# Attention by pairs of heads in both halves of the rows, with normed probabilities and values summed in PSUM

## The chip, the cores and the metric

The kernel runs on one core of a Trainium2 chip. The metric is device time in microseconds (us) of one execution; every program is executed several times and the median counts. TensorE (PE) multiplies matrices from SBUF into PSUM, VectorE (DVE) and ScalarE (ACT) work element by element, GpSimd (POOL) here issues gathers by index, SyncE (SP) issues the loads of the weights. Each engine works through its own queue in program order, and the queues meet at semaphores.

## The reference, cut to what matters

Two transformer blocks follow each other on 512 tokens of width 1024, in float32.

- The first block has MLA attention (8 heads, 96 wide keys, 16 meta tokens ahead of the sequence), a retention branch, a merge by sigmoid gates, and then PEER: each token picks 128 rows of a table `peer_u` of 16384 rows, takes the dot product of each with its activations, and adds 128 rows of a table `peer_v`, weighted, to the residual.
- The second block has a pooling branch, an attention of three branches (NSA), gates, and an MLP of width 4096.

The NSA part is the larger share of what is changed:

```
s = jnp.where(mask, (q @ k.T) * scale, -1e30); p = where(mask, softmax(s), 0)
o_c = p_c @ v_cmp          # compressed keys: at most 31, one softmax
o_s = p_s @ v_sel          # with 512 tokens every block is selected: causal attention
o_w = p_w @ v_win          # the window holds all 512 tokens: causal attention
o = g[0] * o_c + g[1] * o_s + g[2] * o_w    # 16 heads, 2 groups of keys, head width 64
```

The MLA part is `o = softmax(mask(q @ k.T * scale)) @ v` for 8 heads of value width 64.

## The kernel before

The 512 tokens are four tiles of 128. `first_wave` (L1766) runs the first block on tiles 0 and 1 (run 0) and on tiles 2 and 3 (run 1). `second_wave` (L1925) runs the second block on tiles 0 and 1 (run 0), tile 2 (run 1) and tile 3 (run 2). Within a wave the stages follow one another (norm, products, rope, turning, attention, merge, MLP). A stage begins on an engine once the last work of the stage before has ended on all engines (`open`, `begin`). Weights stream through a ring of three slabs of 2 MB, loaded by SP.

The PEER picks of the first block are spread over later stages. There are 1024 steps of VectorE (4 tiles, 128 rows of `peer_u` and 128 of `peer_v` each). Each step needs one gather of 128 rows of 4 KB, issued by POOL (L306) into one of 8 buffers. `SHARES` says how many steps each stage takes, and `g.picks.use(dve)` puts a stage's steps evenly between its own instructions on VectorE. Tiles 0 and 1 must be complete (512 steps) before run 0 of the second wave, tile 2 (892 steps) before run 1 and tile 3 (1024) before run 2. Run 2 of the second wave has no picks. `on_pe` is False for all, so that VectorE does each of them: L363 for `peer_u`, L369 for `peer_v`.

`attention_stage` (L784 to L953) takes a list of items. An item is one head, one query tile and one branch. Its steps are:

- TensorE: scores (L835, queries stationary), one more product that adds the mask (L836, identity times a causal bias), for MLA also 16 meta columns (L840).
- VectorE: the maximum of the scores (L931). ScalarE: exponential with the sum of the row (L890). VectorE: for the compressed branch a product with `seen` (L936).
- TensorE: transposes of the unnormed probabilities, 128 keys each (L875). ScalarE: copies them to SBUF (L899, L902).
- TensorE: values, the turned probabilities stationary (128 columns), the values moving (64 columns) (L865). Each item has its own sum in PSUM.
- VectorE: reciprocal of the sums (L911), gate (L913), and then factor times values, added to the head's output (L918, L920).

The output has tokens in the rows, so that one more `turn_stage` ("to") turns it for the merge. Item i's scores lie in one of three banks (in one of two places where there are more than 512 keys, which is called wide, tile 3 of MLA). For NSA a head's items are compressed, selected, window. There are 48 items for a tile of the second wave and 8 for one of the first. The keys of a tile t are 128 (t + 1) in number.

## Time and profile before

| | us |
|---|---|
| time, median of 3 runs | 3436.53 (3432.90 to 3439.03) |
| profiled execution, own time | 3432.37 |
| its span | 3431.0 |
| PE busy | 2454.4 (72%) |
| DVE busy | 1890.6 (55%) |
| ACT busy | 456.1 (13%) |
| POOL busy | 1311.4 (38%) |
| gathers (queue q0) | 148416 packets, 539.79 MB for 1024 gathers |
| weight loads (queue q1) | 283.19 MB |

The span is from the first to the last instruction of the program. Busy shares are averages over stages with different limits, so that they say little by themselves. The mean granted TensorE clock over the span is 0.734 of full speed. Full speed is 2.4 GHz and the lower level is 1.2 GHz.

### The profile page before, as it was taken

The page shows a single profiled execution, that of the slowest core. Times are in us where ns is not written, and L with a number is a line of the kernel's source. Part 1 is how long each engine was busy: PE and PEld are TensorE (multiplying, and loading weights), DVE is VectorE, ACT ScalarE, POOL GpSimd, SP SyncE. Part 2 cuts the span into 40 slices and gives each one's busy share as a digit, 9 for nine tenths or more (in the row PEclk, how much of TensorE's full clock was granted, in tenths as well). Part 3 has the DMA queues.
Part 4 walks back from the last instruction along what each step waited for, and adds up shares of the span by engine and source line. Part 5 has one row for each costly group of instructions (what it writes and reads, how often), then busy time and mean ns, then how long its engine had stood idle before and what let it go on. Part 6 is the DMA issues. An engine that isn't in the chain of part 4 may idle for free. (4 is left out here: it accounts for less than half of the span.)

```text
span 3431.0 us, 24950 instructions
## 1 busy us (share of the span) xinstructions
PE 2454.4 (72%) x8300; PEld 1594.3 (46%) x8300; DVE 1890.6 (55%) x3669; ACT 456.1 (13%) x1214; POOL 1311.4 (38%) x1041
## 2 busy tenths in 40 slices
PE   6998930365847543003959998897679979799989
PEld 3547630234526522002647686763356534466544
DVE  1511169887676778997777656666554442212100
ACT  1201000012101000000023210110122100122110
POOL 0000004767466877347664345885431241000000
PEclk9998965685767866555855579999755789855699
DMA  4221406898688999669897569999863699510176
GB/s 138 92 85 65 162 21 196 308 384 294 225 338 285 402 331 363 194 209 335 327 352 226 174 234 400 371 401 401 308 228 90 212 398 336 189 37 0 63 268 226
DMA packets 291711, 829.17 MB, mean 242 GB/s; under 512 B 23568, under 2 KB 30144, under 8 KB 290816
## 3 DMA queue, kind: packets, MB, share of 16 engines
q0 software_dynamic: 148416, 539.79, 43.8%
q1 hardware_dynamic: 139872, 283.19, 22.7%
q10 hardware_dynamic: 3296, 4.60, 0.4%
q8 instruction: 67, 1.10, 0.1%
q14 instruction: 60, 0.49, 0.0%
HBM read 825.40 MB, written 2.10 MB: 241 GB/s over the span
## 5 line engine op out<-in xcount | busy, mean ns | idle before, releaser
L306 POOL DMA_INDIRECT picks_rows<-peer_u_dram,expert x512 | 698.2, 1364 | 821.0 <-DVE expert L1441 506.1
L306 POOL DMA_INDIRECT picks_rows<-peer_v_dram,expert x512 | 605.7, 1183 | 770.1 <-DVE h L369 655.6
L363 DVE CUSTOM_DVE_ANT_0 picks_rows<-picks_rows,xn 128x1024 f32<-128x1024 f32 x512 | 616.7, 1223 | 178.8 <-DMA picks_rows<-peer_u_dram,expert 173.7
L369 DVE SCALAR_TENSOR_TENSOR h<-picks_rows,picks_weight,h 128x1024 f32<-128x1024 f32 x512 | 655.0, 1279 | 101.5 <-ACT aT L2031 47.7
L637 PE MATMUL psum<-identity_sb,n_scaled 128*128 128x128 f32 (+1 forms) x104 | 23.6, 405 | 327.0 <-DVE n_scaled L622 327.0
L447 PE MATMUL psum<-weight_ring,hnT 128*128 128x512 f32 (+4 forms) x576 | 238.6, 576 | 23.5 <-DMA weight_ring<-w_in_dram 11.9
L1727 PE MATMUL psum<-weight_ring,aT 128*128 128x512 f32 x512 | 224.4, 600 | 8.6 <-DMA weight_ring<-w_ff_dram 6.4
L931 DVE TENSOR_REDUCE na_negmax<-psum 128x1 f32<-128x15 f32 (+6 forms) x192 | 74.3, 387 | 254.6 <-PE psum L836 254.4
L835 PE MATMUL psum<-nsa_kT_sb,qT 64*128 64x128 f32 (+3 forms) x256 | 181.2, 809 | 0.0
L447 PEld LDWEIGHTS psum<-weight_ring,hnT 128*128 128x128 f32 (+1 forms) x576 | 106.9, 188 | 153.8 <-issue 140.4
L637 PEld LDWEIGHTS psum<-identity_sb,n_scaled 128*128 128x128 f32 (+1 forms) x104 | 19.4, 218 | 332.7 <-issue 293.0
L1727 PEld LDWEIGHTS psum<-weight_ring,aT 128*128 128x128 f32 x512 | 97.8, 192 | 133.6 <-issue 121.0
L865 PE MATMUL psum<-nsa_kv_sb,na_probsT 128*128 128x64 f32 x640 | 157.3, 413 | 0.0
L865 PEld LDWEIGHTS psum<-nsa_kv_sb,na_probsT 128*128 128x128 f32 x640 | 151.5, 333 | 0.0
L447 PE MATMUL psum<-weight_ring,mergedT 128*128 128x512 f32 x256 | 115.6, 613 | 36.0 <-DVE mergedT L1192 34.6
L836 PEld LDWEIGHTS psum<-causal_sb,identity_sb 128*128 128x128 f32 x320 | 78.9, 296 | 121.7 <-issue 120.3
L1387 PE MATMUL psum<-keysT_sb,pqT 64*128 64x128 f32 x128 | 11.7, 352 | 172.4 <-DVE gates_sb L1447 171.5
L1309 PE MATMUL psum<-weight_ring,xn 128*128 128x512 f32 x256 | 120.3, 627 | 14.7 <-DMA weight_ring<-w_ff_dram 9.7
L890 ACT ACTIVATE na_probs<-psum,na_negmax 128x15 f32<-128x15 f32 (+6 forms) x192 | 85.2, 444 | 328.2 <-DVE na_negmax L931 327.9
L875 PE MATMUL psum<-identity_sb,na_probs 128*128 128x128 f32 (+2 forms) x384 | 125.3, 430 | 0.8 <-ACT na_probs L890 0.8
L447 PE MATMUL psum<-xn,weight_ring 128*128 128x256 f32 x512 | 113.0, 384 | 7.2 <-DVE xn L603 7.2
L1157 PE MATMUL psum<-hnT,weight_ring 128*128 128x256 f32 x512 | 115.6, 388 | 1.6 <-DVE oT L693 0.9
(357 smaller groups left out, 3422.4 us busy)
## 6 DMA issues: line engine op xcount, KB each, us to landing
weight_ring<-w_ff_dram SPq DMA_DIRECT2D x48, 2048.0 KB, 16.0
weight_ring<-w_in_dram SPq DMA_DIRECT2D x44, 2048.0 KB, 13.2
weight_ring<-w_proj_nsa_dram SPq DMA_DIRECT2D x6, 2048.0 KB, 7.9
weight_ring<-w_out_dram SPq DMA_DIRECT2D x6, 2048.0 KB, 18.7
weight_ring<-w_ret_out_dram SPq DMA_DIRECT2D x4, 2048.0 KB, 7.9
weight_ring<-w_mix_out_dram SPq DMA_DIRECT2D x4, 2048.0 KB, 18.2
weight_ring<-w_peer_q_dram SPq DMA_DIRECT2D x4, 2048.0 KB, 13.2
picks_rows<-peer_u_dram,expert POOLq DMA_INDIRECT x512, 9.3
```

The source lines that it names most:

```text
L306: pool.indirect_dma_start(out=self.rows[:, n % GATHERS, :], out_offset=None, in_=table, in_offset=bass.IndirectOffsetOnAxis(ap=self.expert ...
L363: ins = nc.vector.tensor_tensor_reduce(out=row, in0=row, in1=self.x[t], scale=1.0, scalar=0.0, op0=ALU.mult, op1=ALU.add, accum_out=self.d ...
L369: ins = nc.vector.scalar_tensor_tensor(out=h, in0=row, scalar=self.weight[:, t % 2, k:k + 1], in1=h, op0=ALU.mult, op1=ALU.add)
L447: mm = g.nc.tensor.matmul(g.psum[0:rows, n % BANKS, 0:cols], lhsT, rhs, start=(k == 0), stop=(k == len(pairs) - 1))
L835: nc.tensor.matmul(scores(i)[:, at:end], it.q, it.kT, start=True, stop=False)
L836: return nc.tensor.matmul(scores(i)[:, end - it.bias.shape[1]:end], g.identity[:], it.bias, start=False, stop=True)
L865: mm = nc.tensor.matmul(values(j), probsT[0:keys, j % 2, P * m:P * m + P], v, start=(m == 0), stop=(m == last))
L875: mm = nc.tensor.transpose(turned(j, m, keys), probs[:, j % depth, col:col + keys], g.identity[:])
L890: nc.scalar.activation(probs[:, i % depth, 0:items[i].keys], scores(i), ACT.Exp, bias=negmax[:, i % 4:i % 4 + 1], accum_out=rowsum[:, i % ...
L1157: mm = nc.tensor.matmul(g.psum[0:rows, n % BANKS, 0:cols], lhsT, rhs, start=(k == 0), stop=(k == len(pairs) - 1))
L1309: mm = nc.tensor.matmul(g.psum[:, n % 3, :], lhsT, rhs, start=(k == 0), stop=(k == len(pairs) - 1))
L1727: mm = nc.tensor.matmul(g.psum[:, n_tiles * b + t, :], aT[:, KT * k + i, P * t:P * t + P], w[:, i, :], start=(k == 0 and i == 0), stop=(k ...
```

## The change

- Items come in pairs: heads h and h + 1 of the same branch. For NSA the even head's queries and keys lie in SBUF rows 0 to 63, the odd head's in rows 64 to 127 (queries are turned two heads at a time, keys are turned twice).
- Queries are scaled by a negative number. One VectorE instruction (`tensor_tensor_reduce`) adds the mask to the scores in PSUM, in place, and takes their minimum. The product with the bias on TensorE is gone. ScalarE takes exp(-s + minimum).
- VectorE norms the probabilities in SBUF (reciprocal, then times factor and gate) ahead of the transposes.
- In the value products the values are stationary (64 columns) and the turned probabilities move (128 columns). The output comes out turned, head h in half h % 2 of the rows, and the three branches are summed in PSUM. A set of 8 heads (for MLA one tile's 8 heads) is evacuated by one ScalarE copy. The "to" stages are gone.
- Scores have four banks (two pairs) and probabilities four buffers. The wide case keeps two places.
- `SHARES` has new numbers: for run 1 of the first wave and `sel2`, `sel3` the sum stays 460, for run 0 and run 1 of the second wave 380 and 132. `compress_stage` and `mlp_down_stage` put picks at more places. `Picks.fold` and the extra `picks.add` calls do nothing here, since `on_pe` stays False.

```diff
 SHARES = {
-    "sel1": 24, "n1_1": 14, "lat_1": 19, "nq_1": 9, "nkv_1": 10, "up_1": 19, "qk_1": 19, "tq_1": 5, "tk_1": 6, "ma2_1": 28,
-    "ma3_1": 28, "rp_1": 43, "tr_1": 7, "re_1": 19, "rn_1": 8, "to_1": 4, "m1_1": 71, "mix_1": 24, "np_1": 14, "pq_1": 28,
-    "sel2": 43, "sel3": 42, "drain_0": 28, "n22_0": 8, "u2_0": 9, "pool2_0": 6, "q2_0": 17, "kc2_0": 8, "kv2_0": 11,
-    "cmp2_0": 31, "tq2_0": 4, "tk2_0": 2, "na2_0": 89, "to2_0": 3, "m2_0": 42, "out2_0": 13, "n32_0": 9, "ff12_0": 61,
-    "ff22_0": 60, "nf2_0": 7, "n22_1": 2, "u2_1": 4, "pool2_1": 2, "q2_1": 6, "kc2_1": 3, "kv2_1": 3, "cmp2_1": 17,
-    "tq2_1": 2, "tk2_1": 1, "na2_1": 29, "to2_1": 1, "m2_1": 16, "out2_1": 4, "n32_1": 3, "ff12_1": 18, "ff22_1": 19,
-    "nf2_1": 2}
+    "sel1": 24, "n1_1": 13, "lat_1": 13, "nq_1": 9, "nkv_1": 9, "up_1": 12, "qk_1": 16, "tq_1": 6, "tk_1": 5, "ma2_1": 26,
+    "ma3_1": 27, "rp_1": 35, "tr_1": 7, "re_1": 58, "rn_1": 9, "m1_1": 55, "mix_1": 18, "np_1": 22, "pq_1": 18, "sel2": 51,
+    "sel3": 51, "drain_0": 28, "n22_0": 11, "u2_0": 7, "pool2_0": 11, "q2_0": 14, "kc2_0": 9, "kv2_0": 15, "cmp2_0": 41,
+    "tq2_0": 7, "tk2_0": 3, "na2_0": 81, "m2_0": 46, "out2_0": 14, "n32_0": 11, "ff12_0": 50, "ff22_0": 49, "nf2_0": 11,
+    "n22_1": 4, "u2_1": 3, "pool2_1": 5, "q2_1": 5, "kc2_1": 3, "kv2_1": 4, "cmp2_1": 24, "tq2_1": 3, "tk2_1": 1,
+    "na2_1": 35, "m2_1": 10, "out2_1": 3, "n32_1": 5, "ff12_1": 11, "ff22_1": 12, "nf2_1": 4}
...
+def turn_twice(g, bank, columns, src, rows):
+    for part in (0, HD):
+        mm = g.nc.tensor.matmul(g.psum[part:part + HD, bank, columns], src, g.identity[0:rows, 0:rows], start=True, stop=True)
+    return mm
...
-def attention_stage(g, tag, items, head_dim, group):
+def attention_stage(g, tag, items, outputs):
...
-    depth = 2 if wide else 3
+    depth = 2 if wide else 4
...
+        def score(pe, s):
+            for i in pair(s):
+                it = items[i]
+                if i >= depth:
+                    pe.wait_ge(*s_exp.after(i - depth + 1))
+                    if wide:
+                        pe.wait_ge(*s_copied.after(i - depth + 1))
+                mm = nc.tensor.matmul(scores(i)[:, 0:it.kT.shape[-1]], it.q, it.kT, start=True, stop=True)
+                if it.meta is not None:
+                    mm = nc.tensor.matmul(scores(i)[:, it.kT.shape[-1]:it.keys], it.q, it.meta[0], start=True, stop=True)
+                mm.then_inc(s_scores.sem, 1)
+        def turn(pe, s):
+            for j in pair(s):
+                pe.wait_ge(*s_normed.after(j + 1))
+                if j >= 2:
+                    pe.wait_ge(*s_copied.after(j - 1))
+                for m, (at, keys, _) in enumerate(items[j].blocks):
+                    mm = nc.tensor.transpose(turned(j, m, keys), probs[:, j % 4, at:at + keys], g.identity[:])
+                mm.then_inc(s_turned.sem, 1)
+        def value(pe, s):
+            for j in pair(s):
+                it = items[j]
+                pe.wait_ge(*s_copied.after(j + 1))
+                if it.set >= 2 and items[j - 1].set < it.set:
+                    pe.wait_ge(*s_out.after(it.set - 1))
+                for m, (_, keys, v) in enumerate(it.blocks):
+                    mm = nc.tensor.matmul(values(j), v, probsT[0:keys, j % 4, P * m:P * m + P], start=it.start and m == 0,
+                                          stop=it.stop and m == len(it.blocks) - 1)
+                mm.then_inc(s_values.sem, 1)
...
+            for s in range(steps + 2):
+                if wide:
+                    turn(pe, s - 1)
+                    score(pe, s)
+                else:
+                    score(pe, s)
+                    turn(pe, s - 1)
+                value(pe, s - 2)
...
+            for s in range(steps + 4):          # ScalarE
+                if wide:
+                    copies(act, s - 1)
+                    exponentials(act, s)
+                else:
+                    exponentials(act, s)
+                    copies(act, s - 1)
...
+            for s in range(steps):              # VectorE
+                for i in pair(s):
                     dve.wait_ge(*s_scores.after(i + 1))
+                    nc.vector.tensor_tensor_reduce(out=scores(i), in0=scores(i), in1=items[i].mask, scale=1.0, scalar=-LOWEST,
+                                                   op0=ALU.add, op1=ALU.min, accum_out=least[:, i % 8:i % 8 + 1]).then_inc(s_least.sem, 1)
+                g.picks.use(dve)
+                for i in pair(s):
+                    it, p = items[i], probs[:, i % 4, 0:items[i].keys]
+                    f = factor[:, i % 8:i % 8 + 1]
+                    dve.wait_ge(*s_exp.after(i + 1))
+                    if it.seen is not None:
+                        nc.vector.tensor_tensor(p, p, it.seen, ALU.mult)
+                    link(nc.vector.reciprocal(f, rowsum[:, i % 8:i % 8 + 1]))
+                    if it.gate is None:
+                        ins = nc.vector.tensor_scalar(p, p, f, None, ALU.mult)
+                    else:
+                        ins = nc.vector.tensor_scalar(p, p, f, it.gate, ALU.mult, ALU.mult)
+                    ins.then_inc(s_normed.sem, 1)
                 g.picks.use(dve)
...
-                turn_stage(g, tag("tq"), [([q[:, j, HD * h:HD * h + HD] for h in range(h0, h0 + 4)], P,
-                                           qT[:, h0:h0 + 4, P * j:P * j + P]) for j in range(n) for h0 in range(0, NH, 4)],
-                           HD, scale=HD ** -0.5)
+                turn_stage(g, tag("tq"), [([q[:, j, P * c:P * c + P] for c in range(c0, c0 + 4)], P,
+                                           qT[:, c0:c0 + 4, P * j:P * j + P]) for j in range(n) for c0 in (0, 4)],
+                           P, scale=-HD ** -0.5)
...
-        turn_stage(g, tag("to"), [([o[:, j, P * c:P * c + P] for c in range(c0, c0 + 4)], P, oT[:, c0:c0 + 4, P * j:P * j + P])
-                                  for j in range(n) for c0 in (0, 4)], P)
```

## Rows read from the trace of the kernel before

**Rows 1.** Page, second part: granted clock in tenths, 40 slices of 85.8 us.

```profile
PEclk9998965685767866555855579999755789855699
```

**Rows 2.** Windows: us; PE, PEld, DVE, ACT, POOL busy (count); clock, DMA share, GB/s.

```profile
122.80:153.90 31.10, 29.65 (x217) 26.61 (x217) 11.10 (x40) 16.51 (x65) 0.00 (x0) 1.00 0.01 5
768.50:836.70 68.20, 40.03 (x147) 31.36 (x148) 51.05 (x68) 13.93 (x36) 52.42 (x40) 0.55 0.90 313
836.70:902.90 66.20, 47.91 (x167) 37.26 (x165) 43.03 (x48) 11.36 (x32) 35.51 (x28) 0.50 0.67 223
1765.70:1999.00 233.30, 232.16 (x768) 165.20 (x768) 166.30 (x412) 73.80 (x292) 90.72 (x92) 0.51 0.68 211
2527.20:2695.40 168.20, 167.04 (x528) 111.92 (x529) 73.97 (x175) 48.51 (x146) 28.09 (x30) 0.51 0.34 102
3025.50:3228.00 202.50, 201.33 (x625) 132.65 (x626) 44.31 (x144) 55.40 (x146) 0.00 (x0) 0.51 0.00 1
```

**Rows 3.** Timeline, last attention stage: start, us, engine, instruction, idle before.

```profile
3105.06 0.69 ACT L890 ACTIVATE na_probs<-psum,na_negmax 128x512 f32<-128x512 f32 x1 [2.87 <-DVE na_negmax L931]
...
3106.04 0.63 PE L835 MATMUL psum<-k_cmpT_sb,qT 64*128 64x31 f32 x2
...
3107.05 1.95 PE L865 MATMUL psum<-nsa_kv_sb,na_probsT 128*128 128x64 f32 x8
3108.79 1.06 PE L875 MATMUL psum<-identity_sb,na_probs 128*128 128x128 f32 x4
3109.78 2.07 PE L835 MATMUL psum<-nsa_kT_sb,qT 64*128 64x512 f32 x2
3111.78 0.80 PE L836 MATMUL psum<-causal_sb,identity_sb 128*128 128x128 f32 x2
```

**Rows 4.** Timeline after the last attention: the merge's first product.

```profile
3230.83 2.04 PE L1238 MATMUL psum<-weight_ring,h2T 128*128 128x512 f32 x2 [0.93 <-DVE oT L693]
```

**Rows 5.** VectorE groups by form: count, busy us, mean ns, idle before.

```profile
L363 DVE DVE_READ_ACCUMULATOR2_ANT picks_dots<- 128x1 f32 x512 | 41.5, 81 | 0.0
L931 DVE TENSOR_REDUCE na_negmax<-psum 128x1 f32<-128x512 f32 x32 | 22.1, 690 | 98.1 <-PE psum L836 98.1
L911 DVE RECIPROCAL na_factor<-na_rowsum 128x3 f32<-128x3 f32 x64 | 10.8, 169 | 0.0
L622 DVE TENSOR_SCALAR n_scaled<-h,n_inverse 128x1024 f32<-128x1024 f32 x12 | 9.0, 751 | 0.2
L622 DVE TENSOR_SCALAR nkv_scaled<-ckv,nkv_inverse 128x256 f32<-128x256 f32 x4 | 1.4, 345 | 0.0
```

**Rows 6.** Page, fifth part: the two instructions of the picks.

```profile
L363 DVE CUSTOM_DVE_ANT_0 picks_rows<-picks_rows,xn 128x1024 f32<-128x1024 f32 x512 | 616.7, 1223 | 178.8 <-DMA picks_rows<-peer_u_dram,expert 173.7
L369 DVE SCALAR_TENSOR_TENSOR h<-picks_rows,picks_weight,h 128x1024 f32<-128x1024 f32 x512 | 655.0, 1279 | 101.5 <-ACT aT L2031 47.7
```

**Rows 7.** Timeline of TensorE: retention's products by halves of columns and rows.

```profile
1011.67 1.49 PE L1027 MATMUL psum<-rv,rk 128*64 128x128 f32 x12
1013.09 2.08 PE L1011 MATMUL psum<-xn 64*128 64x128 f32 x16
```

**Rows 8.** Windows with the clock: compression, turning of queries, the stretch after.

```profile
1703.70:1757.30 53.60, 19.40 (x100) 18.99 (x100) 39.44 (x72) 0.59 (x3) 43.45 (x33) 0.50 1.03 404
...
1757.40:1761.40 4.00, 4.00 (x20) 3.33 (x21) 3.93 (x7) 2.24 (x4) 3.39 (x3) 0.50 1.03 411
1761.50:1768.20 6.70, 4.92 (x34) 3.78 (x32) 3.57 (x8) 4.53 (x9) 5.17 (x6) 1.00 1.01 388
```

**Rows 9.** Windows: retention run 1, merge run 1, MLP run 1, selection of tiles 2, 3.

```profile
997.70:1050.00 52.30, 29.05 (x112) 20.90 (x112) 36.26 (x74) 7.50 (x19) 23.63 (x20) 0.50 0.57 196
1067.10:1208.60 141.50, 104.69 (x450) 87.64 (x450) 94.78 (x169) 7.42 (x17) 107.74 (x73) 0.87 0.99 376
2782.00:2909.70 127.70, 110.77 (x258) 49.60 (x259) 49.23 (x41) 8.79 (x16) 41.18 (x33) 0.92 0.96 358
...
1327.80:1523.10 195.30, 3.79 (x32) 3.52 (x32) 190.17 (x489) 1.59 (x2) 94.13 (x87) 0.50 0.74 243
```

313 lines of the change are left out of this document (135 added, 178 removed).

## The prediction

> **What bounds the kernel now.** I read the granted clock in slices first, then windows of each attention stage, then the order of instructions inside the longest one, then the stages that hold the picks. Counted from 1, slices 21 to 23, 30, 31, 36 and 37 have the clock at half, among others [rows 1], and these are the three NSA attentions. The windows say how they are bound [rows 2]. The three NSA stages take 233.3, 168.2 and 202.5 us, 604 us or 18% of the span, TensorE is busy in all but 1 us of each, and the clock is 0.51, which is the 1.2 GHz level. VectorE is busy 71%, 44% and 22% of them. The MLA stages take 31.1 us (clock 1.00) and 68.2 + 66.2 us, in which picks on VectorE and TensorE take turns.
>
> Inside the last NSA stage [rows 3] an item with 512 keys costs on TensorE 2.00 us of scores, 0.6 of mask, 1.0 of transposes and 1.74 to 1.95 of values, some 5.5; a compressed item costs about 1.6. A head is two of the first and one of the second, 12.7 us, and 16 heads are 203 us, as the window has it. The value products are short of work: 64 moving columns for 128 loaded ones, so that each key block costs 0.22 us per instruction, the time of its load; in this window the loads alone are busy 132.65 us [rows 2].
>
> Elsewhere there are two kinds of stage, which matter for the new shares [rows 9]. In the merge and the MLP of run 1 the DMA share is 0.99 and 0.96: a gather more is 0.527 MB (539.79 MB / 1024) at about 400 GB/s, 1.31 us. In the selection VectorE is busy 190 of 195 us: a step more is what it costs there, 1.22 + 0.08 us for peer_u [rows 5, 6] or 1.28 us for peer_v [rows 6], I take 1.34 with the few hundredths between two.
>
> **The change part by part, at the low clock first.** *Mask product.* It goes: 0.6 us per item of 512 keys.
>
> *Scores.* Two heads stand in different halves of the rows. Eight score products of 128 columns that alternate so in the retention take 2.08 us in 16 instructions [rows 7]; an instruction with 512 moving columns takes 0.87 at the low clock (2.00 us for two, less 0.25 of loading [rows 3]), one with 128 a quarter, so that the 16 would take 3.5 us one after the other. Neighbours in different halves overlap, those in the same half do not. A pair has only two products of two parts each: part two of the first runs beside part one of the second, so that three of four parts are paid. At 512 keys: 3 × 0.87 + 0.25 for the first load = 2.85 us, against 4.0 [rows 3]. Without overlap it is 3.7; with full overlap 2.0. I take 2.85. MLA has 96 rows and gets nothing.
>
> *Transposes.* As before, 4 in 1.06 us [rows 3], 2.2 us for the pair.
>
> *Values.* 128 columns now move past 64 loaded ones, the form of the retention's products into halves of columns, 12 instructions in 1.49 us where halves alternate [rows 7], which is 0.25 us per product. Here the blocks of one head follow each other in one half. Bounds per block are 0.25 and 0.44 us (today's two instructions); I take 0.44, since only one boundary in eight changes the half. 8 × 0.44 = 3.5 us for the pair, no gain at the low clock, but the engine now streams all the time instead of waiting for loads.
>
> So a pair at 512 keys costs 8.6 us against 11.1, a compressed pair about 2.6 against 3.2 (0.63 us for the score [rows 3], less its mask), two heads 19.8 against 25.3. At the low clock the last stage would be 8 × 19.8 + 3 = 161 us.
>
> *The clock.* Does it stay low? In today's attention and in the compression (30 to 62 moving columns behind loads of 128, clock 0.50 over 53.6 us [rows 8]) the engine mostly waits for loads. Just after the compression the queries are turned, transposes of 128 moving columns behind 64 loaded, PE busy 4.00 of 4.00 us, and the clock goes from 0.50 to 1.00 in the next stretch [rows 8]. The new value products have that same shape. MLA run 0 keeps clock 1.00 with 29.65 of 31.10 us busy [rows 2]. I take it that the last NSA stage and the one before it run at the high level. The Trainium skill says otherwise of part of this work (TensorE: Matmul & The Clock Gate, Part 4): transposes in PE mode do not count as activity that lifts the clock. This trace speaks against it by the 0.50 to 1.00 above; if the page were right, the low clock of the first rival would be likelier than I have it.
>
> *VectorE.* The pass with the mask is not in the trace in this form (PSUM in and out). From below it is the reduction of 512, 0.69 us, from above one picks step of 1024 elements, 1.30 us [rows 5, 6]; I take 0.69 + 0.08 for the accumulator, and 1.04 ns less per element below 512. Norming is a reciprocal, 0.17, and a product in SBUF: 0.345 us for 256 and 0.751 for 1024 elements [rows 5] give 0.21 + n/1.9 ns, 0.48 at 512. With `seen` on the compressed items, 0.17 more, two heads of own VectorE work come to 7.9, 7.1, 6.2 and 5.5 us for 4, 3, 2 and 1 key blocks. Output factors and additions go.
>
> **Stage by stage.** *NSA, run 2* (no picks): at the high clock TensorE needs 9.9 us per two heads. A step on VectorE is pass, exponential (0.69 us [rows 3] and 0.19 for its sum), norm: 3.3 us at 512 keys, 8.6 per two heads with the serial waits, and it runs beside the transposes and values of the pairs before. TensorE sets the pace: 8 × 9.9 + 6 of filling and draining = 85 us, −117.
>
> *NSA, run 1*: 35 picks × 1.34 = 47 and 8 × 7.1 = 57 on VectorE, 104 us; TensorE needs 63 at the high and 126 at the low clock. VectorE sets the pace: 112 us, −56.
>
> *NSA, run 0*: 81 × 1.34 = 109 and 8 × (6.2 + 5.5) = 94, 203 us, and 7 for waits; TensorE at the low clock needs 8 × (11.8 + 8.5) = 162, hidden. 210 us, −23.
>
> *MLA, run 1*: tile 2, own work and 26 picks, 4 periods of 11.3 plus filling, 50 us. Tile 3 is wide: no scores of the next pair before this pair's copies, 4 × 13 + 10 = 62. Together 112 against 134.4, −22. *MLA, run 0*: 4 × 2.1 (VectorE with its waits for the exponential) + 4 × 3.0 (TensorE) + 5 = 25.5, −5.6.
>
> *"to" stages.* The last one puts the merge 3 us after the window's end at 3228.0 [rows 4]. Five of them with their picks apart: −2.4 (run 0), −4.4, −2.6, −2.9, and one of 4 picks in run 1, below. Turning queries in pairs saves 1 us in the last run; keys turned twice cost 0.6 each, hidden but there.
>
> *New shares.* Until `sel3` 65 steps move: 58 go from stages bound by the DMA or by TensorE with it (1.3 us each, −75), 4 with "to" (−4.6), 3 from attention (counted); retention takes 39 (+40: today 52.3 us with VectorE busy 36.3 [rows 9], then 58 × 1.34 + 12.7 = 90), selection 17 (+23), norms 9 (+12). Net −5. Run 0: compression takes 10 at DMA share 1.03 (+13 [rows 8]), other small stages 28 (+23, many beside TensorE), while MLP and products give 27, of which only the second MLP half is held by the DMA (−20): +16. Run 1: +20 for compression and small stages, −22 for merge and MLP, whose 127.7 us are 37 gathers and 32 MB of weights at 400 GB/s [rows 9]; 14 fewer leave 113: −2.
>
> **Sum.** Start −8. First wave run 1 −22 − 5 = −27. Second wave run 0: −23 − 4.4 + 16 = −11. Run 1: −56 − 2.6 − 2 = −61. Run 2: −117 − 2.9 − 1 = −121. Together −228 us. The profiled execution had 3432.4 us with a span of 3431.0; it would have 3204. The median of before is 4 us above it, 3436.5, so I forecast 3208.
>
> **Rivals.**
> 1. *The clock stays low.* For it: all three NSA stages had it low with TensorE busy throughout [rows 2]. Against it: the rise on transposes. Run 2 161 instead of 85, run 1 128 instead of 112: 3208 + 92 = 3300.
> 2. *The shares give nothing back.* Stages that lose picks are held by their products, while those that get picks pay in full. For it: the merge has TensorE busy 104.7 of 141.5 us and the MLP 110.8 of 127.7 [rows 9]. Against it: their DMA shares. The give-backs are 75 + 20 + 20: up to 3323.
> 3. *The hand-over becomes serial (slower).* Each pair goes VectorE, ScalarE, VectorE, TensorE, ScalarE, TensorE, and picks stand in front of the norm. If TensorE waits for normed probabilities at every step, its time adds to VectorE's instead of lying beneath it: run 0 203 + 162 (+155 on my value), run 1 104 + 126 (+118), run 2 63 + 158 (+136), MLA +30: 3208 + 439 = 3647. It decides (3436) once half of TensorE's work is uncovered. Against it: four score banks hold two pairs, and between scores and transposes of a pair lie some 4 us of other TensorE work at the high clock, more than the 3.3 us that are waited for.
> 4. *More comes back than I count*, as whole stages have slack today (first wave run 1 above all): 60 us more, 3148.
>
> **Chances.** Forecast 0.60, rival 1 0.15, rival 2 0.11, rival 3 0.03, rival 4 0.11. The forecast's own range is 3160 to 3250; eight in ten needs both neighbours: 3130 to 3305. A difference of 0.2% (7 us) is about what a measurement of this kernel can tell from no change. Faster 0.95, same 0.01, slower 0.04.
>
> **What would show it.** The windows of the three NSA attentions near 210, 112 and 85 us; clock about 1.00 in the last; no line for the mask product; score pairs starting within one part of each other; the pass over 512 scores near 0.77 us; retention of run 1 near 90 us and merge of run 1 near 120. I am wrong if the last attention takes over 130 us, if TensorE there idles before the transposes, or if the time saved in attention reappears in stages that got picks.

## The result and the profile after

| | us | ratio to before, 95% interval |
|---|---|---|
| before, median | 3437.78 | |
| after, median of 4 runs (3161.86 to 3182.18) | 3173.71 | 0.9228 (0.9193 to 0.9262) |
| after, 6 more runs beside the experiments (3157.44 to 3183.50) | 3172.89 | 0.9217 (0.9177 to 0.9257) |

The change makes the kernel 7.7% faster, 264 us. The forecast was 3208, the range 3130 to 3305. The six further runs are called the control below. The profiled execution of after took 3182.18 us with a span of 3180.8, 250 less than the span of before. Its clock in slices, which stands against [rows 1], and its windows of the five attention stages, then of retention and merge in run 1 (columns as in [rows 2]):

```profile
PEclk9787995577585896655585557989987698986999
```

```profile
121.90:172.30 50.40, 48.58 (x184) 32.68 (x184) 13.50 (x64) 15.89 (x67) 0.00 (x0) 0.54 0.01 4
751.20:874.90 123.70, 76.08 (x280) 51.66 (x280) 93.03 (x155) 26.08 (x69) 88.85 (x64) 0.57 0.85 294
1774.10:1957.60 183.50, 118.35 (x576) 62.06 (x576) 170.69 (x520) 63.37 (x296) 120.83 (x92) 0.53 0.81 263
2481.70:2579.80 98.10, 73.04 (x432) 45.86 (x432) 86.73 (x244) 41.12 (x148) 41.08 (x37) 0.74 0.69 211
2891.50:2980.50 89.00, 79.06 (x528) 53.22 (x528) 54.01 (x208) 48.23 (x147) 0.00 (x0) 0.83 0.00 1
...
956.70:1047.90 91.20, 29.05 (x112) 20.91 (x112) 85.62 (x116) 7.50 (x19) 65.65 (x57) 0.50 0.92 334
1059.20:1172.80 113.60, 99.37 (x448) 86.89 (x449) 72.90 (x131) 7.41 (x17) 82.83 (x58) 0.94 0.99 375
```

Set against [rows 2], this is where the time went, in this profile and in the control's, which shows the same kernel in another execution:

| stage | before | forecast | after | control |
|---|---|---|---|---|
| MLA run 0 | 31.1 | 25.5 | 50.4 | 45.7 |
| MLA run 1 | 134.4 | 112 | 123.7 | 115.0 |
| NSA run 0 | 233.3 | 210 | 183.5 | 181.3 |
| NSA run 1 | 168.2 | 112 | 98.1 | 97.9 |
| NSA run 2 | 202.5 | 85 | 89.0 | 85.9 |
| the five together, difference | | -225 | -225 | -244 |
| all the rest, difference | | -3 | -25 | -16 |

That forecast and profile agree at -225 is chance: the five terms are off by +25, +12, -27, -14 and +4 us, which cancel, and the control's sum is another.

TensorE was the bound of all three NSA stages. Now VectorE is that of run 0 (busy 170.7 of 183.5) and run 1 (86.7 of 98.1), and in run 2 nobody is busy throughout: TensorE 79 of 89 us, VectorE 54.

The rest comes apart by the starts and ends of the windows. From MLA run 0 to MLA run 1 it is 614.6 us before and 578.9 after (fewer picks there), from MLA run 1 to NSA run 0 862.8 and 899.2 (more picks), from the end of NSA run 1 to the start of run 2 330.1 and 311.7. Retention in run 1 went from 52.3 to 91.2 us and the merge to 113.6, as the picks moved: near 90 and 120 were forecast.

### The profile page after: what moved, and what is told of

It is laid out like the page before. It is cut to its first block and busy times, and to the rows that moved or that the text cites. A ratio compares the mean times of both kernels' runs of the same rounds, so it can differ in the third digit from the quotient of the medians.

```text
span 3180.8 us, 23856 instructions
## 1 busy us (share of the span) xinstructions
PE 2103.0 (66%) x7838; PEld 1321.1 (42%) x7838; DVE 1912.1 (60%) x3970; ACT 425.6 (13%) x1209; POOL 1346.1 (42%) x1041
## 3 DMA queue, kind: packets, MB, share of 16 engines
q8 instruction: 63, 1.03, 0.1%
## 5 line engine op out<-in xcount | busy, mean ns | idle before, releaser
L315 POOL DMA_INDIRECT picks_rows<-peer_v_dram,expert x512 | 636.3, 1243 | 561.7 <-DVE h L380 451.4
L874 PE MATMUL psum<-identity_sb,na_probs 128*128 128x128 f32 (+2 forms) x384 | 93.7, 360 | 99.8 <-DVE na_probs L958 78.5
L1333 PE MATMUL psum<-weight_ring,xn 128*128 128x512 f32 x256 | 118.8, 621 | 11.6 <-DVE xn L621 7.4
L874 PEld LDWEIGHTS psum<-identity_sb,na_probs 128*128 128x128 f32 (+2 forms) x384 | 48.8, 160 | 161.2 <-DVE na_probs L958 148.6
L945 DVE CUSTOM_DVE_ANT_0 psum<-psum,mask_sb 128x128 f32<-128x128 f32 (+7 forms) x160 | 76.5, 514 | 57.2 <-PE psum L865 33.7
L907 ACT ACTIVATE na_probs<-psum,na_least 128x15 f32<-128x15 f32 (+6 forms) x192 | 83.5, 440 | 193.6 <-DVE na_least L945 193.5
L1181 PEld LDWEIGHTS psum<-hnT,weight_ring 128*128 128x128 f32 x512 | 100.2, 196 | 20.0 <-ACT xn L1140 5.8
L465 PEld LDWEIGHTS psum<-xn,weight_ring 128*128 128x128 f32 x512 | 98.5, 193 | 22.7 <-issue 9.3
```

What stands on the lines that cost most here:

```text
L315: pool.indirect_dma_start(out=self.rows[:, n % GATHERS, :], out_offset=None, in_=table, in_offset=bass.IndirectOffsetOnAxis(ap=self.expert ...
L465: mm = g.nc.tensor.matmul(g.psum[0:rows, n % BANKS, 0:cols], lhsT, rhs, start=(k == 0), stop=(k == len(pairs) - 1))
L874: mm = nc.tensor.transpose(turned(j, m, keys), probs[:, j % 4, at:at + keys], g.identity[:])
L907: nc.scalar.activation(probs[:, i % 4, 0:items[i].keys], scores(i), ACT.Exp, bias=least[:, i % 8:i % 8 + 1], scale=-1.0, accum_out=rowsum[ ...
L945: nc.vector.tensor_tensor_reduce(out=scores(i), in0=scores(i), in1=items[i].mask, scale=1.0, scalar=-LOWEST, op0=ALU.add, op1=ALU.min, acc ...
L1181: mm = nc.tensor.matmul(g.psum[0:rows, n % BANKS, 0:cols], lhsT, rhs, start=(k == 0), stop=(k == len(pairs) - 1))
```

## The experiments

All times are medians, and each ratio is to the kernel before on the same chip. Ratios from different chips are compared with their intervals. A window of a stage is cut as in [rows 2], from TensorE's first product of it to its end.

**New shares alone**, in the kernel before.

```diff
 SHARES = {
-    "sel1": 24, "n1_1": 14, "lat_1": 19, "nq_1": 9, "nkv_1": 10, "up_1": 19, "qk_1": 19, "tq_1": 5, "tk_1": 6, "ma2_1": 28,
+    "sel1": 24, "n1_1": 13, "lat_1": 13, "nq_1": 9, "nkv_1": 9, "up_1": 12, "qk_1": 16, "tq_1": 6, "tk_1": 5, "ma2_1": 26,
...
```

> The kernel before with nothing changed but SHARES, which take the changed kernel's numbers. Theory (as in the prediction): stages that lose picks and stages that get them nearly cancel, -5 and +16 and -2 us by the prediction's sum, and the picks that move in or out of the NSA attentions cost nothing there, as TensorE sets the pace of those stages in the kernel before. So 3437 + 9 = 3446 us, at most 20 either way. Rival 1: the new shares are a large part of the gain by themselves, 40 us or more faster than before. Rival 2: they only fit the new attention, and the old one with them is 40 us or more slower.

Measured: 3441.83 us, ratio 1.0001 (0.9972 to 1.0031). The theory holds; the new shares alone give nothing beyond 10 us. But the profile showed something else. Window of MLA run 0:

```profile
119.60:172.90 53.30, 52.23 (x216) 45.68 (x216) 10.83 (x39) 16.80 (x65) 0.00 (x0) 0.52 0.01 4
122.80:172.90 50.10, 50.08 (x198) 43.60 (x198) 9.90 (x36) 15.02 (x62) 0.00 (x0) 0.50 0.00 1
```

The attention here is the old one, instruction for instruction, and it took 53.3 us at clock 0.52, where the profile of before has 31.1 at 1.00 [rows 2]. The second line leaves out the first 3.2 us: from there on the clock is 0.50, though TensorE is busy in all 50 us. In both, TensorE waits 1.03 us for the first probabilities. Timeline of TensorE, first in this run, then in the kernel before:

```profile
122.82 0.69 PE L868 MATMUL psum<-identity_sb,ma_probs 128*128 128x128 f32 x2 [1.03 <-ACT ma_probs L883]
123.30 0.64 PE L828 MATMUL psum<-mla_kT,xn 96*128 96x128 f32 x2
```

```profile
125.96 0.44 PE L875 MATMUL psum<-identity_sb,ma_probs 128*128 128x128 f32 x2 [1.03 <-ACT ma_probs L890]
126.24 0.39 PE L835 MATMUL psum<-mla_kT,xn 96*128 96x128 f32 x2
```

The same instructions take 0.69 and 0.64 us in one execution, 0.44 and 0.39 in the other. The products ahead of the gap took 0.46 and 0.39 us in both, so that the high clock ended in the gap. So the level of this stage differs between executions of the same instructions, for a reason that no run shows, and is worth 22 us. The one profile that the prediction had showed the good side of it; a third profile of the old attention, of the run without its mask product below, has 46.9 us at 0.54.

**Old shares in the changed kernel.**

```diff
 SHARES = {
-    "sel1": 24, "n1_1": 13, "lat_1": 13, "nq_1": 9, "nkv_1": 9, "up_1": 12, "qk_1": 16, "tq_1": 6, "tk_1": 5, "ma2_1": 26,
+    "sel1": 24, "n1_1": 14, "lat_1": 19, "nq_1": 9, "nkv_1": 10, "up_1": 19, "qk_1": 19, "tq_1": 5, "tk_1": 6, "ma2_1": 28,
...
```

> The changed kernel with the shares of the kernel before (those of the 'to' stages, 8 steps, go to the norm after the retention, 4, and to the merges, 3 and 1). Theory: NSA attention of run 0 gets 8 steps of 1.3 us more and is set by VectorE (+10), that of run 1 gets 6 fewer (-8), MLA of run 1 3 more (+4), and the rest nearly cancels as the prediction's sum has it (+5 - 16 + 2 = -9): 3174 us, at most 25 either way. Rival: the new shares are what turns a shorter attention into a shorter kernel, and without them 50 us or more come back.

Measured: 3177.96 us, 0.9233 (0.9176 to 0.9291), as the changed kernel, with an interval of 20 us to either side. The shares don't matter beyond that in this attention either.

**Both heads in one row half.**

```diff
-            qT = alloc(nsa, tag("qT"), [P, NH // 2, width])
+            qT = alloc(nsa, tag("qT"), [HD, NH, width])
...
-                                half = slice(HD * (h % 2), HD * (h % 2) + HD)
+                                half = slice(0, HD)
```

> The changed kernel, but all NSA queries and keys lie in rows 0 to 63, so that the scores of a pair of heads stand in the same half of the rows. All else is as in the changed kernel (queries are turned in pieces of 64 columns, as before). Theory: score products of a pair stop overlapping; four instructions of 512 columns take 1.7 to 1.8 us at the high clock instead of 1.13, and 3.5 to 3.7 at the low one instead of 2.07. In the last stage TensorE is most of the pace, 16 pairs of 512 and 8 compressed ones give +10 to +13 us; in the two stages with picks VectorE hides most of it, +0 to +8. 3174 + 16 = 3190 us. Rival 1: TensorE waits for the norm anyway, 1.2 to 1.8 us in each cycle of two heads, and the longer scores only fill that wait: within 5 us of the changed kernel. Rival 2: the extra busy time raises the granted clock, and the kernel is faster.

Measured: 3190.22 us, 0.9263 (0.9204 to 0.9321). That is +12 us on the changed kernel's 0.9228, but the intervals overlap, so the stages have to decide. Timeline of TensorE in the last NSA stage, the score pair at the low clock and at the high one, in this run and then in the changed kernel:

```profile
2900.12 3.78 PE L863 MATMUL psum<-nsa_kT_sb,qT 64*128 64x512 f32 x4
...
2937.32 1.98 PE L863 MATMUL psum<-nsa_kT_sb,qT 64*128 64x512 f32 x4
```

```profile
2895.89 2.08 PE L863 MATMUL psum<-nsa_kT_sb,qT 64*128 64x512 f32 x4
...
2916.07 1.13 PE L863 MATMUL psum<-nsa_kT_sb,qT 64*128 64x512 f32 x4
```

In the changed kernel the pair takes 1.13 us at the high clock, and 2.06 to 2.08 at the low one: the two heads' products run wholly beside each other, so that two parts of four are paid and not three. Without the overlap the last stage took 92.2 us (after 89.0, in the control 85.9) and NSA of run 1 109.5 (98.1 and 97.9). The second is more than the theory has: the clock is 0.59 there instead of 0.74, TensorE is busy 102 us instead of 73, and VectorE waits 15 us for scores instead of 4. NSA of run 0 didn't suffer, since VectorE sets its pace (below).

**Value blocks of a pair in turn.**

```diff
             for j in pair(s):
                 it = items[j]
                 pe.wait_ge(*s_copied.after(j + 1))
...
-                for m, (_, keys, v) in enumerate(it.blocks):
-                    mm = nc.tensor.matmul(values(j), v, ...
+            for m in range(len(items[2 * s].blocks) if pair(s) else 0):
+                for j in pair(s):
+                    mm = nc.tensor.matmul(values(j), v, ...
```

> The changed kernel, but the value products of a pair go block by block, first head, second head, first head, and so on, so that neighbours write different column halves of the array (different rows of PSUM); for MLA the two 16-row meta blocks stand beside each other. Theory: products of different column halves overlap as in the retention (12 in 1.49 us at the low clock, 0.125 us each, is the best that could come); 16 instructions at 512 keys go from 1.58 us at the high clock and 2.88 at the low one to some 1.1 and 2.0, and the last NSA stage, in which TensorE is busy 79 of 89 us, loses 5 to 8 us; MLA run 0, at the low clock with 0.62 us per alternation of 128 rows and 16, loses 3 to 5. Together 3174 - 10 = 3164 us. Rival 1: the products don't overlap any further, they are bound by their loads, and nothing moves (within 3 us). Rival 2: the pair's first products now wait for both heads' copies on ScalarE, and the kernel is 5 us or more slower.

Measured: 3151.12 us, 0.9151 (0.9080 to 0.9223), -26 us on the changed kernel by the ratios, where -10 was expected; the intervals overlap. The five stages take 502 us together, against 545 in the changed kernel's first profile and 526 in the control's, but not all of that is the edit's: NSA of run 0 lasts 173.9 us from the first mask pass of VectorE on, to the tenth as in both of those, and its window is 9 or 7 us shorter only since no pick of earlier stages stands in front. Timeline of TensorE, a pair's values in the changed kernel (512 keys at the low clock and at the high one; MLA run 0, blocks of 128 rows and of 16, at the low clock), then here:

```profile
2903.04 2.88 PE L885 MATMUL psum<-na_probsT,nsa_kv_sb 128*64 128x128 f32 x16
...
2914.56 1.58 PE L885 MATMUL psum<-na_probsT,nsa_kv_sb 128*64 128x128 f32 x16
...
129.07 2.54 PE L885 MATMUL psum<-ma_probsT,mla_v 128*64 128x128 f32 x8
```

```profile
125.97 1.32 PE L888 MATMUL psum<-ma_probsT,mla_v 128*64 128x128 f32 x8
...
2914.86 1.09 PE L888 MATMUL psum<-na_probsT,nsa_kv_sb 128*64 128x128 f32 x16
```

Products that alternate between column halves overlap further. MLA run 0 went from 50.4 us (45.7 in the control) to 38.8, at the low clock (0.53). Its eight products took 2.54 us and now take 1.32. Two things changed for them: column halves alternate, and the two 16-row blocks stand beside each other. That the change between 128 and 16 rows is dear by itself is seen in the changed kernel alone: a pair's sixteen products with 128 rows take 2.88 us at the same clock, 0.18 each, and these eight 0.32 each. The last NSA stage went to 84.8, 1 us below the control, where 5 to 8 were expected: what TensorE saves there it waits for, as the next run shows. The Trainium skill (TensorE: Matmul & The Clock Gate, Part 3: Packing small matmuls, "The mechanism") says that loads overlap running products only where the row groups differ. Here all rows are the same and only the column halves differ, and 1.58 us became 1.09, so that neighbours gain without a difference in rows; whether their loads or the products themselves overlap, no row here tells.

**Minima one pair ahead**, on top of the run before.

```diff
+                    if s == 0:
+                        score(pe, 0)
-                    score(pe, s)
+                    score(pe, s + 1)
                     turn(pe, s - 1)
...
+                    g.picks.activate(act, min(2 * s + 1, 2 * steps))
...
+            for s in range(steps):
+                minima(s)
+                g.picks.use(dve)
+                norms(s if wide else s - 1)
+                g.picks.use(dve)
```

> The kernel of the run 'alternate' with one more change: VectorE takes the minima of pair s + 1 ahead of norming pair s, and TensorE forms scores one pair earlier (four banks already hold two pairs). Nothing is added or left out; tile 3 of MLA (wide) is as before. Theory: in the last NSA stage neither TensorE nor VectorE sets the pace alone but the loop minimum, exponential, norm, minimum of the next pair: about 1.4 + 0.2 + 1.7 us of waiting per step of 3.2. With the loop cut TensorE is the bound, about 8 us for two heads: the stage goes from 84.9 to about 72 us, the NSA stages with picks lose 3 to 8 us each, MLA 3. 3151 - 22 = 3129 us. Rival 1: TensorE is the bound already, and nothing moves (within 4 us). Rival 2: the stages with picks get slower, as norms now stand behind one more pass of VectorE: 5 us or more slower.

Measured: 3126.59 us, 0.9115 (0.9095 to 0.9136). Windows of NSA run 1 and run 2:

```profile
2454.50:2546.40 91.90, 71.69 (x432) 42.05 (x432) 85.73 (x244) 44.53 (x146) 40.92 (x37) 0.72 0.73 229
2855.00:2925.90 70.90, 66.67 (x528) 40.59 (x528) 51.03 (x208) 50.06 (x146) 0.00 (x0) 0.89 0.00 1
```

The last stage takes 70.9 us (expected 72), with TensorE busy 66.7. So the loop minimum, exponential, norm and next minimum was its pace, and the forecast's "TensorE sets the pace" was wrong for it. The stages with picks gained 3 to 4 us: run 1 91.9 against 94.6, and run 0 169.7 against 173.9 from the first mask pass on (its whole window, 176.8 against 174.6, has six picks of earlier stages in front, that of 'alternate' none). MLA of run 1 took 122.2 us where 'alternate' had 109.4, so that only 12 us are left by the ratios, whose intervals overlap; the same stage took 123.7 and 115.0 in two executions of the changed kernel, and whether the new order costs there is open.

**Two more products in MLA run 0**, in the changed kernel.

```diff
+                    if tag == "ma0_0" and s == 1:
+                        for _ in range(2):
+                            nc.tensor.matmul(g.psum[:, 7, :], g.identity[:], g.h[:, 0, 0:512], start=True, stop=True)
                     turn(pe, s - 1)
```

> The changed kernel with two more products on TensorE (identity times 512 columns of h, into a bank that nobody reads), in the MLA attention of run 0 alone, ahead of the first transposes, where TensorE is idle for 1.67 us and the clock then falls from 1.00 to 0.50. Theory: the idle stretch is what ends the high clock; with it filled the stage stays at 1.00, and takes about 35 us instead of 50.2: 3174 - 14 = 3160 us. Rival 1: the stage's own products are too thin to hold the clock and it falls anyway; the stage stays at 50 or gets 1 us longer. Rival 2: the clock stays high but the stage is bound elsewhere (alternating blocks of 128 rows and 16), 45 us.

Measured: 3155.71 us, 0.9190 (0.9167 to 0.9213). Window of the stage:

```profile
121.80:151.90 30.10, 29.74 (x188) 20.49 (x188) 14.10 (x64) 15.65 (x66) 0.00 (x0) 1.00 0.02 7
```

The clock stays at 1.00, and 50.4 us (45.7 in the control) become 30.1. Work for nothing in a gap of 1.67 us buys back 20 or 16 by the profiles; the times give 13 by the ratios, with intervals that overlap. One execution at 1.00 would prove little, as the old attention had one too. But nine other profiles of the new attention on record have no such products, and all nine show 0.52 to 0.60 in this stage, while the two with them show 1.00 and 0.87 (the second is 'all_three').

**No norming product.**

```diff
-                    link(nc.vector.reciprocal(f, rowsum[:, i % 8:i % 8 + 1]))
-                    if it.gate is None:
-                        ins = nc.vector.tensor_scalar(p, p, f, None, ALU.mult)
-                    else:
-                        ins = nc.vector.tensor_scalar(p, p, f, it.gate, ALU.mult, ALU.mult)
-                    ins.then_inc(s_normed.sem, 1)
+                    nc.vector.reciprocal(f, rowsum[:, i % 8:i % 8 + 1]).then_inc(s_normed.sem, 1)
```

> The changed kernel without the product of probabilities with factor and gate on VectorE (left out: the norm and the gates of the probabilities; the reciprocal stays and releases the transposes). Theory: VectorE sets the pace of the NSA stages with picks, where 96 and 48 such products of 0.3 to 0.55 us go: -30 and -14 us there, -6 in MLA of run 1; in the last stage, with its loop of minimum, exponential and norm, -8. 3174 - 55 = 3119 us. Rival 1: TensorE is the pace in three of four stages, and only 15 us go. Rival 2: with less on VectorE the picks come sooner and wait for their gathers: NSA of run 0 gives 10 us and no more (3174 - 25).

Measured: 3114.32 us, 0.9067 (0.9040 to 0.9094), -55 us as expected. NSA run 0 went from 183.5 to 147.6 us, run 1 from 98.1 to 82.8, run 2 from 89.0 to 80.7 (control 85.9): the norming product costs most where VectorE has picks beside it. MLA run 0 stayed at 49.8 us and clock 0.54. Timeline of TensorE there:

```profile
125.44 1.05 PE L874 MATMUL psum<-identity_sb,ma_probs 128*128 128x128 f32 x4 [1.33 <-DVE ma_factor L954]
```

So without the norming product the gap is 1.33 us and the clock falls all the same.

**Values moving again.**

```diff
...
-                    mm = nc.tensor.matmul(values(j), v, probsT[0:keys, j % 4, P * m:P * m + P], start=it.start and m == 0,
...
+                    mm = nc.tensor.matmul(values(j), probsT[0:keys, j % 4, P * m:P * m + P], v, start=m == 0,
...
```

> The changed kernel with the operands of the value products exchanged back: the turned probabilities (128 columns) are loaded and the values (64 columns) move. The output is left unturned and every branch's product overwrites the last (left out: the turned layout and the sum of branches); all other instructions are the same. Theory (the prediction's): the granted clock rises in the last two NSA stages because 128 columns now move past 64 loaded ones; with 64 past 128 it stays at 0.50 to 0.55, and the last stage takes 8 x (4.6 scores + 5.0 transposes + 8.0 values) = 140 us and more instead of 88.9, NSA of run 1 about 120 instead of 98, that of run 0, set by VectorE, +0 to +10: 3174 + 80 = 3254 us. Rival 1: the clock rises anyway (the mask product with its short second part is gone, or for another reason), and only the longer products cost: 8 blocks of 0.22 against 0.10 to 0.20 us, +1 us in each pair, +20 us in the last stage: 3174 + 30 = 3204. Rival 2: orientation gives nothing, as TensorE waits for the norm anyway: within 5 us.

**Both shapes undone**, this and the one row half together.

> The changed kernel with the edits of 'one_half' and 'values_moving3' together: all NSA queries and keys in rows 0 to 63, and the turned probabilities loaded with the values moving (left out, as there: the turned layout and the sum of branches). Each alone left the last NSA stage at a high clock in its profile (0.90 and 0.91, 92 and 87 us), while the kernel before without its mask product stayed at 0.50 (176.6 us) with nearly the same products on TensorE. Theory: either of the two shapes (two score products at once, or values with 128 moving columns) is enough to raise the clock, and with both undone it stays at 0.50: the last stage takes 8 x 21.6 = 173 us, NSA of run 1 some 140, run 0 +10: 3215 + 130 = 3345 us. Rival: the shapes of the products don't decide; something in the order of pairs or in the short waits of TensorE does, and the clock rises here too: last stage 92 to 98 us, NSA of run 1 +10: 3235 us. In between: the level differs from execution to execution, and the times scatter by 50 us or more.

**The kernel before without its mask product.**

```diff
-            nc.tensor.matmul(scores(i)[:, at:end], it.q, it.kT, start=True, stop=False)
-            return nc.tensor.matmul(scores(i)[:, end - it.bias.shape[1]:end], g.identity[:], it.bias, start=False, stop=True)
+            return nc.tensor.matmul(scores(i)[:, at:end], it.q, it.kT, start=True, stop=True)
```

> The kernel before without the product that adds the mask (left out: the mask). Everything else is as before, single heads, unnormed probabilities, values moving. The question is whether this product is what kept the clock of the NSA stages at 0.51. Theory: it is not; what keeps it low is that every product of these stages is short beside its load, the values above all, and the clock stays at 0.50 to 0.52. Then only the products' own time goes: 0.6 us for each of 32 items of 512 keys and 0.3 for 16 compressed ones, -24 us in each of run 2 and run 1 and -48 in run 0, -8 in MLA: 3437 - 104 = 3333 us. Rival: without it the clock rises as in the changed kernel, the last stage takes some 110 us instead of 202.5 and NSA of run 1 130 instead of 168: 3437 - 210 = 3225 us or less.

Windows of the last NSA stage in these three, in this order:

```profile
2905.90:2992.70 86.80, 78.53 (x528) 60.03 (x528) 54.69 (x208) 47.78 (x146) 0.00 (x0) 0.91 0.00 1
```

```profile
2943.00:3106.40 163.40, 163.36 (x528) 116.23 (x528) 57.03 (x208) 52.08 (x146) 0.00 (x0) 0.50 0.00 1
```

```profile
2970.20:3146.80 176.60, 176.56 (x528) 111.53 (x528) 44.09 (x143) 54.78 (x145) 0.00 (x0) 0.50 0.00 1
```

| | values 64 columns past 128 | values 128 columns past 64 |
|---|---|---|
| scores of a pair in one half | 3299.51 us, 0.9586 (0.9556 to 0.9616); last stage 0.50 | 3190.22, 0.9263; 0.90 |
| scores of a pair in two halves | 3215.09 us, 0.9376 (0.9352 to 0.9399); 0.91 | 3173.71, 0.9228; 0.83 |

Values moving took 3215.09 us where the theory had 3254: the clock rose in the last stage all the same, as that run's first rival had it (3204). Both undone took 3299.51 us where 3345 was expected, with 163.4 us for the last stage (173 expected). The clock of the last stage stays at 0.50 only where both are undone. Either shape is enough to raise it there, and so the forecast's reason (the shape of the values) is one of two. In NSA of run 1 each counts: the clock is 0.74 with both shapes, 0.59 without the two halves, 0.53 with the values moving and 0.50 without either, and the stage takes 98.1, 109.5, 107.5 and 129.9 us. The effects don't add: two halves are worth 72 us with the one shape of the values and 12 with the other, the values' shape 111 us with the scores in one half and 51 with them in two. For values moving, the profiled execution, 3193.46 us, was the fastest of four, the others took 3212.69 to 3223.32; in which stage these were longer isn't shown. Without the mask the old kernel took 3347.65 us, 0.9721 (0.9670 to 0.9772): -96 us (-104 expected), at the low clock as the theory had it.

These runs make a ladder from the kernel before to the changed one: -96 us for the mask product, -46 to the kernel with both shapes undone (pairs, mask pass, norm and evacuation by sets, new shares, no "to" stages), -111 for the values' shape, -12 for the two halves. In another order the last two steps have other sizes, as said.

**All three together**: value blocks in turn, minima ahead, two more products.

> The kernel of 'pipelined3' (value blocks of a pair in turn, minima one pair ahead) with the two extra products of 'filler3' in the MLA attention of run 0. Theory: they don't overlap in time and add up, but in 'pipelined3' the MLA stage of run 0 took 34.4 us and can go to some 27 with the clock at 1.00: 3127 - 8 = 3119 us, ratio to before 0.909. Rival: scores one pair earlier have already shortened the idle stretch, and the extra products only cost their 2 us: 3128.

Measured: 3121.59 us (3113.72 to 3125.42), 0.9074 (0.9039 to 0.9110). Window of MLA run 0:

```profile
118.80:146.00 27.20, 26.01 (x188) 18.64 (x188) 13.24 (x64) 15.13 (x66) 0.00 (x0) 0.87 0.02 5
```

Nothing is left out of it, and it is 51 us below the changed kernel on the same chip. How much of that comes on top of 'pipelined3' is not settled, as the intervals overlap. Timeline of TensorE at the start of the stage:

```profile
121.89 0.79 PE L863 MATMUL psum<-mla_kT,xn 96*128 96x128 f32 x2 [1.14 <-ACT ma_probs L916]
...
123.61 3.76 PE L905 MATMUL psum<-h,identity_sb 128*128 128x512 f32 x4
...
128.35 0.29 PE L865 MATMUL psum<-mla_kT,xn 96*128 96x16 f32 x2
```

Here the clock fell in a gap of 1.14 us ahead of the added products, these ran at the low level (3.76 us, in 'filler3' 1.96), and behind them it was high again: the meta product takes 0.29 us and not 0.45.

> The changed kernel once more, unchanged, as a control beside the others on one chip. Theory: 0.9228 of before, 3170 us, within 0.3%, with the clock falling to 0.50 in the MLA attention of run 0 in most executions (some 50 us for that stage). Rival: its level there differs from execution to execution, as it did between the two profiles of the old attention (31.1 us at 1.00 and 53.3 at 0.52), and the times scatter by 20 us.

Measured: 3172.89 us, 0.9217; in its profile MLA run 0 took 45.7 us at clock 0.59, and NSA of run 2 85.9 at 0.87. The levels do differ somewhat from execution to execution, and the times scatter by 26 us.

## Why the prediction was right, and where it was not

*Mask product.* Right: 0.6 us per item of 512 keys, which is 24 us in each of run 1 and run 2. Measured in the kernel before: 168.2 to 142.2 and 202.5 to 176.6 (26 each), 233.3 to 187.1 in run 0; 96 us in all, the first step of the 264.

*Scores.* The mechanism was right, the size was not: 2.06 to 2.08 us at the low clock where 2.85 was taken. "Part two of the first runs beside part one of the second" was too careful; the lower bound that was named, 2.0, is what came.

*Values.* A pair's 16 instructions at 512 keys took 2.88 us at the low clock, 0.36 per block and not 0.44, and 1.58 at the high one, 0.20 per block.

*VectorE.* Here the terms were too large, and this is the term of the sum that was mis-sized most. Timeline of VectorE in NSA run 0: the first pick and the first mask pass in the window, then the first mask pass in 'alternate', whose window begins at 1762.8:

```profile
1774.23 1.23 DVE L374 CUSTOM_DVE_ANT_0 picks_rows<-picks_rows,xn 128x1024 f32<-128x1024 f32 x1 [0.80 <-DMA picks_rows<-peer_u_dram,expert]
...
1783.73 0.17 DVE L945 CUSTOM_DVE_ANT_0 psum<-psum,cmp_mask_sb 128x15 f32<-128x15 f32 x1
```

```profile
1763.54 0.18 DVE L949 CUSTOM_DVE_ANT_0 psum<-psum,cmp_mask_sb 128x15 f32<-128x15 f32 x1 [6.05 <-PE psum L863]
```

In the changed kernel six picks of earlier stages stand in front, 9.6 us with their waits for gathers, and behind them the stage takes 173.9 us, with its own 81 picks. It takes 173.9 as well in the control, in 'alternate', 'one_half' and 'filler3', whatever their products on TensorE cost: VectorE sets the pace there. A pair with 128 keys between two picks:

```profile
1849.87 1.28 DVE L380 SCALAR_TENSOR_TENSOR h<-picks_rows,picks_weight,h 128x1024 f32<-128x1024 f32 x1
1851.06 0.29 DVE L945 CUSTOM_DVE_ANT_0 psum<-psum,mask_sb 128x128 f32<-128x128 f32 x1
1851.27 0.14 DVE L945 DVE_READ_ACCUMULATOR2_ANT na_least<- 128x1 f32 x1
1851.27 0.33 DVE L945 CUSTOM_DVE_ANT_0 psum<-psum,mask_sb 128x128 f32<-128x128 f32 x1
1851.52 0.14 DVE L945 DVE_READ_ACCUMULATOR2_ANT na_least<- 128x1 f32 x1
1851.94 0.17 DVE L954 RECIPROCAL na_factor<-na_rowsum 128x1 f32<-128x1 f32 x1 [0.28 <-ACT na_probs L907]
1852.14 0.39 DVE L958 TENSOR_SCALAR na_probs<-na_probs,na_factor,branch_gates 128x128 f32<-128x128 f32 x1
1852.45 0.15 DVE L954 RECIPROCAL na_factor<-na_rowsum 128x1 f32<-128x1 f32 x1
1852.64 0.35 DVE L958 TENSOR_SCALAR na_probs<-na_probs,na_factor,branch_gates 128x128 f32<-128x128 f32 x1
1852.90 1.28 DVE L380 SCALAR_TENSOR_TENSOR h<-picks_rows,picks_weight,h 128x1024 f32<-128x1024 f32 x1
```

The picks that lie in the window of that stage, by form:

```profile
L380 DVE SCALAR_TENSOR_TENSOR h<-picks_rows,picks_weight,h 128x1024 f32<-128x1024 f32 x71 | 90.8, 1279 | 0.0
L374 DVE CUSTOM_DVE_ANT_0 picks_rows<-picks_rows,xn 128x1024 f32<-128x1024 f32 x16 | 19.4, 1220 | 3.1 <-DMA picks_rows<-peer_u_dram,expert 3.0
```

A pick lasts 1.28 us, but the next instruction starts after 1.19, and the accumulator's read (0.14) lies under the next pass. The prediction added durations, 1.34 per step, where the distances of starts count. The 87 picks at 1.19 are 103.5 us; the forecast had 81 of them and 109 us. VectorE was idle for 12.8 us, where 7 were foreseen. What is left of 183.5 is its own work, 67 us and not 94, and that is the term that was mis-sized. The mask pass is a large part of it: at 128 keys the forecast's formula gives 0.37 us, and the second pass starts 0.21 after the first. And by the forecast's own prices two heads come to 5.7 and 4.9 us for 2 and 1 key blocks, where it has 6.2 and 5.5, so that 8 of the 27 us have no source in it. At 512 keys it lasts 0.71 us (0.77 forecast). The same error stands in run 1, 112 against 98.1.

*MLA run 1.* 112 forecast, 123.7 and 115.0 measured. The window opens with eight picks of earlier stages, which take 13.0 and 13.3 us ahead of the first mask pass and are not in the forecast. In the first profile TensorE waits 46.9 us before its transposes for normed probabilities, and VectorE 11.6 us for TensorE (6.5 in the control): here the two do take turns in part, as rival 3 feared. No run takes this stage apart.

*Last NSA stage.* 85 forecast, 89.0 measured (85.9 in the control), but by another way. Timeline of TensorE over two heads:

```profile
2911.92 0.41 PE L863 MATMUL psum<-k_cmpT_sb,qT 64*128 64x31 f32 x4
2913.52 1.11 PE L874 MATMUL psum<-identity_sb,na_probs 128*128 128x128 f32 x8 [1.18 <-ACT na_probsT L917]
...
2921.42 0.41 PE L863 MATMUL psum<-k_cmpT_sb,qT 64*128 64x31 f32 x4
```

Two heads take 9.5 us, near the forecast's 9.9, but TensorE waits 1.18 us in them, and 'pipelined3' shows that this wait is the loop through VectorE. And the first 16 us of the stage are still at the low clock. So the nearness of 85 is partly luck. The prediction named "if TensorE there idles before the transposes" as a sign of being wrong, and it came: 1.18 us in front of them for every two heads, 8.7 us in the stage.

*The clock.* It did rise in the last stage (0.83), and it stayed at 0.53 in run 0, as forecast. In run 1 it was 0.74, short stretches of either level, where the high one was assumed; VectorE is busy 86.7 of 98.1 us there. What that level cost in run 1 isn't shown. The reason given was half of it, by the table of four above. The Trainium skill (TensorE: Matmul & The Clock Gate, Part 4) says that transposes don't count as activity that lifts the clock. With both shapes undone the transposes of 128 columns are all still there and the clock is 0.50, so that in attention they did not lift it: this is on the page's side, where [rows 8] spoke against it.

*MLA run 0*, "clock 1.00", -5.6 us: the step that failed, +19.3 in the profiles. The forecast read one execution's level as a property of the stage. Timeline of TensorE:

```profile
125.58 1.11 PE L874 MATMUL psum<-identity_sb,ma_probs 128*128 128x128 f32 x4 [1.67 <-DVE ma_probs L956]
```

The gap before the first transposes grew from 1.03 to 1.67 us, since the norm now stands in it, and the clock fell in it. That it fell because the gap grew is not shown: it fell after 1.03 us in the old attention with new shares, after 1.14 in 'all_three' and after 1.33 without the norming product, and of all profiles without the added products only that of the kernel before kept it. Against another execution of the old attention (53.3 us) the stage did not get slower at all. The value blocks that change between 128 rows and 16 cost 2.54 us for eight. The clock and the blocks each have a run (30.1 us with the gap filled, 38.8 us with the blocks in turn).

*Shares.* Forecast +9 in sum, measured 0.3 with an interval of 10 to either side. (Its 113 us for the MLP of run 1 is not its own price either: 14 gathers at 1.31 us off 127.7 leave 109.) The rest outside attention, -25 us where -3 was forecast and -16 in the control, is tied to no run, and these two differ by 10 us for the same kernel. In the first profile most of it lies between the end of NSA run 0 and the start of run 2 (-22.5 by the windows), where the merges and MLPs gave up picks.

*The rivals.* The clock did not stay low in run 2, the shares gave back what they took, and the hand-over became serial only in a small form, the 14 us that 'pipelined3' takes off the last stage and the waits in MLA of run 1. "More comes back" (3148) had the right sign: 3174 lies 34 us below the forecast and 26 above that rival. But the slack that it names, in whole stages of run 1 of the first wave, was measured by no run.

## What to carry to other kernels

Sum a busy VectorE by the distance of starts, not by durations. Look at a stage's clock in more than one execution before a forecast rests on its level, and fill a short gap of TensorE in front of a clock-bound stage when nothing else is at hand. Let neighbouring products differ in the half of rows or columns that they use; how much that gives depends on what sets the stage's pace and on its clock (12 us or 72 for the same edit here). Before two windows of a stage are compared, count what of earlier stages lies in them (six picks, 9.6 us, here).

## What was not expected of the hardware

- Two score products in different row halves cost as one: 4 instructions of 512 columns in 1.13 us instead of 1.98 at the high clock, 2.08 instead of 3.78 at the low.
- Products with all rows and alternating column halves also overlap: 16 in 1.09 us instead of 1.58.
- Products that change between 128 and 16 rows take 2.54 us for eight at the low clock, 1.32 when the 16-row blocks stand together and column halves alternate.
- The same 1.03 us gap was followed by the low clock in one execution and by the high one in another; with two products of 512 columns in the gap it stayed high. Once it had fallen it stayed at 0.50 for 50 us with TensorE busy in all of them.
